# Six fixed experts instead of four, with their weight loads partly issued among the last projection loads

## The reference

```python
def hier_moe(h, rg_w, rg_b, re_w, re_b, w_gate, w_up, w_down):
    """h (N,D): top-1 expert group, then top-2 experts inside it"""
    ...
    eid = g_idx * EXPERTS_PER_GROUP + e_idx
    comb = jnp.sum(jax.nn.one_hot(eid, N_EXPERTS, ...) * e_w[..., None], axis=1)
    y = jnp.zeros_like(h)
    for e in range(N_EXPERTS):
        he = jax.nn.silu(h @ w_gate[e]) * (h @ w_up[e])
        y = y + comb[:, e:e + 1] * (he @ w_down[e])
    return y
```

## Time and profile before

| what | value |
|---|---|
| median of the runs | 1071.7 us |
| profiled execution, its own time | 1075.82 us |
| its span | 1074.1 us |
| TensorE busy | 991.3 us (92% of the span) |
| bytes moved by DMA | 226.82 MB |
| last projections with `w_out` | about 220 to 289 us in the span |
| router, then the experts | 289 to 303, 303 to 526 us |

### The profile page before, as it was taken

How to read it: one execution, slowest core, us unless ns; L and a number is a source line. 1 busy time by engine, 2 the same in 40 slices (tenths; PEclk the granted TensorE clock), 3 DMA queues, 4 the chain that set the end, 5 groups by cost and what they waited for, 6 DMA issues and landing times.

```text
span 1074.1 us, 14527 instructions
## 1 busy us (share of the span) xinstructions
PE 991.3 (92%) x5637; PEld 785.2 (73%) x5637; DVE 413.6 (39%) x928; ACT 269.5 (25%) x630; POOL 177.6 (17%) x159
## 2 busy tenths in 40 slices
PE   4979999999899989766799999999999999999997
PEld 4867877788775645443388887888788888788876
DVE  2149762137732212101452461634315246163422
ACT  2122222201311211111228144123002814412301
POOL 5486997700100000000200000000000000000011
PEclk9888999989989999889899999999999999999999
DMA  7883965638989999999834444322343444432211
GB/s 220 257 259 110 262 219 186 206 116 261 421 348 421 420 421 421 420 421 420 298 113 135 149 154 157 99 98 79 118 149 126 140 143 151 156 109 87 87 51 39
DMA packets 138595, 226.82 MB, mean 211 GB/s; under 512 B 6345, under 2 KB 124450, under 8 KB 126234
## 3 DMA queue, kind: packets, MB, share of 16 engines
q1 hardware_dynamic: 136632, 221.15, 57.6%
q0 software_dynamic: 1600, 4.35, 1.7%
q10 hardware_dynamic: 290, 0.34, 0.1%
HBM read 224.76 MB, written 1.06 MB: 210 GB/s over the span
## 4 chain that ended last, share of the span: by engine, by line
PE 79%; SPq 8%; DVE 5%; DMA 4%; ACT 3%; issue 2%; DVEq 0%; ACTq 0%
PE bank L462 27%; PE bank L1068 10%; SPq L1105 7%; PE bank L931 5%; PE bank L907 5%; PE bank L773 4%; PE bank L679 3%; DMA s<-in_w_up 3%; PE bank L946 3%; PE bank L749 2%; PE bank L809 2%; PE bank L788 2%; DMA ring<-in_w_in 1%; PE bank L572 1%; PE bank L961 1%
## 5 line engine op out<-in xcount | busy, mean ns | idle before, releaser
L462 PE MATMUL bank<-hT,ring 128*128 128x256 f32 x1232 | 277.3, 384 | 0.0
L462 PEld LDWEIGHTS bank<-hT,ring 128*128 128x128 f32 x1232 | 233.6, 192 | 38.1 <-issue 7.1
L1068 PE MATMUL bank<-ring,s 128*128 128x256 f32 x512 | 113.0, 383 | 3.3 <-DVE s L1999 3.3
L1068 PEld LDWEIGHTS bank<-ring,s 128*128 128x128 f32 x512 | 98.3, 192 | 17.3 <-DVE s L1999 3.8
L2150 POOL DMA_DIRECT2D s<-in_final_g x1 | 0.6, 594 | 487.8 <-DVE s L1995 487.8
L773 PE MATMUL bank<-s,z 128*32 128x256 f32 (+1 forms) x448 | 64.1, 430 | 8.2 <-DMA s<-in_w_up 4.5
L1782 DVE SCALAR_TENSOR_TENSOR z<-z,bank 128x256 f32<-128x256 f32 x10 | 4.2, 422 | 162.3 <-ACT z L1309 162.2
L2099 POOL TENSOR_TENSOR ring<-ring,csil 128x2048 f32<-128x2048 f32 x17 | 61.3, 3604 | 18.1 <-PE bank L488 17.2
L931 PE MATMUL bank<-ring,hT 128*128 128x256 f32 x256 | 56.1, 380 | 0.0
L907 PE MATMUL bank<-hT,ring 128*128 128x256 f32 x256 | 55.6, 379 | 0.0
L931 PEld LDWEIGHTS bank<-ring,hT 128*128 128x128 f32 x256 | 48.5, 190 | 7.4 <-issue 0.9
(11 more groups left out here) (408 smaller groups left out, 1508.1 us busy)
## 6 DMA issues: line engine op xcount, KB each, us to landing
ring<-in_w_in SPq DMA_DIRECT2D x56, 1024.0 KB, 5.1
ring<-in_w_ada SPq DMA_DIRECT2D x24, 1024.0 KB, 6.0
ring<-in_w_out SPq DMA_DIRECT2D x20, 1024.0 KB, 5.0
s<-in_w_down SPq DMA_DIRECT2D x18, 1024.0 KB, 21.6
s<-in_w_gate SPq DMA_DIRECT2D x15, 1024.0 KB, 25.3
s<-in_w_up SPq DMA_DIRECT2D x13, 1024.0 KB, 24.3
ring<-in_w_up SPq DMA_DIRECT2D x12, 1024.0 KB, 22.2
ring<-in_w_gate SPq DMA_DIRECT2D x10, 1024.0 KB, 24.6
```

The costliest lines, as they stand in the source:

```text
L462: mm = pe.matmul(b[:, 0:T], w[:, (k0 + kb) * CW + m * P:(k0 + kb) * CW + (m + 1) * P], rhs[:, kb, :], start=(kb == 0), stop=(kb == nk - 1))
L1068: mm = pe.matmul(xo[j, tt][:, 0:CW], yT[:, kb, tt * P:(tt + 1) * P], w[:, kb, :], start=(kh == 0 and kb == 0), stop=(kh == 1 and kb == KB ...
```

## The change

`FIXED` goes from 4 to 6 and `HEAVY` from 4 to 2, and the sequence becomes S S S L L H L L L L: three units of fixed experts first, one heavy unit, six light ones as before. So e0 to e17, all 18 loads of the first round, are of fixed experts. Eight of them, e0 to e7, are issued earlier: three after the last projection pair, three after `w_out` 0, two after the first of the last two neighbours `w_ada_2`. The loads and the matmuls are as many as before.

```diff
-FIXED, HEAVY, LIGHT_SLOTS = 4, 4, 32
-SEQUENCE = "SSLHLLHLLL"
+FIXED, HEAVY, LIGHT_SLOTS = 6, 2, 32
+SEQUENCE = "SSSLLHLLLL"
...
+EARLY_LOADS = {10: 3, 8: 3, 3: 2}
...
-            for n, parts in enumerate(chunks):
-                load(n, parts)
-                if n == 1:
-                    load_layer_rows()
...
-            ids = {}
-            for n, (j, c) in enumerate(expert_order):
+            ids, early = {}, []
+
+            def load_expert(n):
+
+                j, c = expert_order[n]
                 if n < NM:
                     for sem_value in overlaid.get(slot[E0 + n], ()):
                         sp.wait_ge(*sem_value)
+                load(E0 + n, [expert_part(ids.get(j, j), c)])
+
+            for n, parts in enumerate(chunks):
+                load(n, parts)
+                for _ in range(EARLY_LOADS.get(NB1 - n, 0)):
+                    load_expert(len(early))
+                    early.append(n)
+                if n == 1:
+                    load_layer_rows()
+
+            for n, (j, c) in enumerate(expert_order):
+                if n < len(early):
+                    continue
                 if j >= FIXED and j not in ids:
                     if not ids:
                         sp.wait_ge(B.free, B.upto("order"))
                     ids[j] = sp.value_load(order[0:1, j:j + 1], min_val=0, max_val=EXPERTS - 1)
-                load(E0 + n, [expert_part(ids.get(j, j), c)])
+                load_expert(n)
```

## The result

The changed kernel is slower, by about 1%: 1081.39 us in the median of four runs against 1071.3 for the kernel before. The ratio on record is 1.0081 (95% interval 1.0051 to 1.011); the two medians alone would give 1.0094. Run again on another occasion it gave 1.0082 (1.0056 to 1.0108). Forecast were 1073.9 us and "the same, near the edge", with a range up to 1079.0, so the median lies above the range. The profiled execution took 1079.08 us, with a span of 1077.4, against 1075.82 and 1074.1 before: only 3.3 us more, so the two single profiles show less than half of what the runs show.

What follows compares the result with a forecast made beforehand. The prediction took expert transfers at about 420 GB/s as the bound, with the end hanging on when the last up matrix, e91, lands. Its terms, -1.4 + 0.5 + 3.1 = +2.2 us, gave 1073.9 us, range 1069.5 to 1079.0.

Steps and rivals of the forecast that it cites:

- the fixed experts' head start is lost in the slots: First three units: transfers wait for TensorE to free slots, so the early loads' head start is lost.
- head start in full: Rival, expert part: it is bytes by rate, so eight loads moved in front save 19.9 us, 1051.8 us; chance 0.10.
- Terms one and two: Expert part: the stream starts 1.4 us earlier (-1.4); the second load after the pause is late (+0.5, between 0 and 1.0).
- e34: Expert load that waits for a slot until unit 2 is done; lands at 362.6 and begins the unbroken stream.
- e35: The next expert load, 2.49 us later, at 365.1 instead of 366.5 before; a gain of 1.4 us.
- the way from e91 to the end: From the last up matrix to the end: the last three units are L before and after, so it is the same.
- e95: Expert load at which the unbroken stream of transfers ends.
- Term three: Before the router: early loads make `w_out` 1 and `w_out` 3 late, +3.1 us through to the end, bounds +1.0 and +4.6.
- The landing of `w_out` 3: Output projection: it lands at 282.0 behind eight expert and nine column loads, 3.5 us late in all.
- The clock: Rival: the clock falls in the waits before `w_out` 1 and `w_out` 3, 2.8 us on top, 1076.7 us; chance 0.18.
- The 0.44 us that VectorE should have given back: Behind `w_out` 3: VectorE does the first of its last two additions beforehand, so 0.44 us goes.
- The rival of the Trainium skill's rule: Loads ahead of `w_out`: column loads move at 2.49 us too, nothing is late, 1070.8 us; chance 0.20.

Runs made afterwards that it cites:

- slots16: The changed kernel without early loads and with 16 expert slots instead of 18 (hT and rxp left out); ratio 1.0048 to the kernel before.
- no_early: The changed kernel with six fixed experts and the new sequence but no load issued early; ratio 1.0009 to the kernel before.
- after_again: The changed kernel run again unchanged, with a second profile; ratio 1.0082 to the kernel before, 59.1 us from the last merge product to unit 0.
- after_4: The changed kernel again, unchanged, one more profile; 55.9 us from the last merge product to unit 0.
- after: The first profile of the changed kernel; the profiled execution took 1079.08 us, 56.8 us from the last merge product to unit 0.
- after_3: The changed kernel again, unchanged, one profile; 57.1 us from the last merge product to unit 0.
- early_fit: The changed kernel with five early loads instead of eight, none behind `w_out` 0; ratio 1.0008 to the kernel before.
- warm_before: The kernel before with overwritten matmuls in two waits, 18 in the router's and 12 in that for the last ups; ratio 0.9989 to the kernel before.

## Why the prediction was wrong

*That the fixed experts' head start is lost in the slots* was right. Almost nothing moved from 306 to 312, the stream is unbroken only from 366, and from U to X the four profiles of the changed kernel average 222.7 us, as before (222.6 and 222.7). `slots16` shows the mechanism with its size. The rival "head start in full" fell with it.

*Terms one and two* (-1.4 + 0.5 us) were a little hopeful. Instead of -0.9 us the measured change from U to X is +0.1 on average in the changed kernel (221.6 to 223.5 us) and +0.8 us in `no_early`. The step that the units of fixed experts take as long as before holds only where the clock stays up. In `after_again` and `after_4` e34 went out 54.1 us after U, as forecast (54.2), and e35 landed 62.8 and 62.7 us after U, where it had been 63.1 and 63.3. In the profiles `after` and `after_3` e34 went out at 55.7 and e35 landed at 64.4 and 64.7. Those 1.6 us are the 32 products that gather the tokens of unit 1, behind unit 0. They stand behind the wait of 1.65 us that the prediction took as one that leaves the clock alone; in the kernel before and then in the profile after:

```profile
313.64 3.57 PE bank L749 x32
...
317.34 0.44 PE L446 MATMUL bank<-ident,z 128*128 128x128 f32 x2 [1.65 <-DVE z L1794]
...
317.78 5.20 PE bank L750 x32
```

It happened in `no_early`, `early_fit` and `slots16` too, and not in either profile of before. The second load after the pause came 1.4 us later than at full rate, not 0.5. Nor was the way from e91 to the end the same each time: in three of the four profiles of the changed kernel TensorE waited once more in front of the last down product, so that the end hung on e95 and not on e91.

*Term three was the step that failed.* It said +3.1 us with 1.0 and 4.6 as ends; measured are 5.7 to 9.4 us in six profiles, 7.0 on average for the changed kernel. It was mis-sized in three places: on average of those four profiles the landing of `w_out` 3 makes up 2.0 us of the 3.9 that were missing, the clock 1.4, and VectorE's share 0.4.

1. The landing of `w_out` 3. Forecast was 282.0 - 253.3 = 28.7 us after M, measured 30.3 to 31.6. The column loads took 3.0 us each, as worked out (2.98): 350 GB/s from 257 to 267. But behind the last projection pair the expert loads didn't start at the full rate; in the profile after, the pair lands at 228.16 + 4.6 = 232.8 and the third expert load at 229.75 + 11.8 = 241.6, 8.8 us for three instead of 7.5. In `after_again` these three took 9.2 us, and `w_out` 2 came 4.0 us behind the load ahead of it. Why these loads were slower isn't shown. The bounds had been put on the column loads alone.
2. The clock. It was a rival with 0.18, priced 2.8 us, deciding from a wait between 1.7 and 3.5 us. In truth it had fallen at one of the two waits or at both in all six profiles of the table: 1.7 to 3.0 us at `w_out` 3 in five of six. It should have been part of the forecast; "a granted clock of 0.5 at 282" was one of the signs of being wrong that the prediction named, and it is there. The point from which it should decide was wrong as well: after waits of 0.55, 0.57, 0.77 and 1.34 us it had fallen, after one of 0.52 and one of 2.98 not, and the same wait of 1.65 us in front of the gather of unit 1 gave both.
3. The 0.44 us that VectorE should have given back. VectorE did do the first addition beforehand, but that shortened nothing: from TensorE's next matmul behind the last `w_out` product, at 285.92 before and 290.23 after, to VectorE's first step of the router (the logits, at 289.24 and 293.55) it is 3.32 us in both.

*The rival of the Trainium skill's rule* (page "DMA: Bandwidth & Descriptors", section Specifications), by which 1 KB rows move at line rate, fell: where column loads queued it was 350 GB/s from 257 to 267 in the profile after, as it had been 352 before, against 421 for expert loads.

*The range* reached 1079.0, and the median was 1081.4. The worst of the named cases, 4.6 + 0.5 - 1.4 and 2.8 for the clock, came to 1078.2; that the landing could be later than the column loads explain was not in it.

*What stays open.* The ratio says 8.7 us (5.5 to 11.8), the medians of the first runs lie 10.1 us apart, and the average of the profiles shows 6.2 us in the span (1079.9 against 1073.7), since M came 1.3 us earlier in them. The rest lies within the scatter of both. Why the clock falls after one short wait and not after another I can't tell from these runs. Nor do I know what lies in the "issue" stretch behind X: it was 4.9 to 5.1 us in the two profiles of before and in `warm_before`, and 5.4 to 6.6 us in all the others. On average it is 0.9 us longer in the changed kernel than before, and no experiment was made on it.

That U to X came out as before is in part chance: it is the average of two profiles in which the clock fell behind unit 0 (223.2 and 223.5 us) and two in which it stayed up (222.5 and 221.6).

## What to carry to other kernels

Loads that are issued early are not free where the queue has deadlines of its own: add up every byte ahead of each deadline at the rate that this kind of load reaches there, leave some 3 us of margin (here `w_out` 3 came 1.6 to 2.9 us later than counted), and price each wait of TensorE with the clock that it may lose behind it. A prefetch brings only what the buffers can hold on to until the consumer, and not the producer, is the slower side again; here all 18 slots were full at 306, and the last two of them came free at 363. And one profile of each kernel, 3.3 us apart, hid a difference of about 9: compare distances between marks in several.

## What the runs showed of the hardware that was not expected

- The granted clock fell behind waits as short as 0.55 us (a block of 16 products then took 5.4 us instead of 3.7) and stayed up behind one of 2.98 us. The wait is only the last idle piece: between the last `w_out` 2 product and the first of `w_out` 3 TensorE also ran sixteen small matmuls, and from the one to the other it was 2.2 us both in `after_3`, where the clock fell, and in `after_4`, where it didn't. With matmuls that are written over put in the waits, it was up in both profiles that had them (3.62 to 3.72 us for the block).
- SP's issues take longer when much is under way, and it begins at fewer loads where these have 1 KB rows: in the profile after, the load at 257.85 took 2.92 us to issue with landings 12.2 us away, some four loads of 3.0 us; in the expert part it is 2.1 us an issue with landings 27.3 us away, some eleven loads of 2.5 us. That this is a limit on what may be under way is my reading; no run tests it, nor do the runs tell short rows from rows that lie far apart.
- After a pause the second load is late: 8.2 us from issue to landing against 4.7 for the one issued 0.43 us before it, 3.9 us apart where 2.5 is the full rate.
